# Retention computed in two blocks of 256 tokens with a decayed state between them

## The reference

```python
CHUNK = 64
q = rotary(...) * (C_HEAD_DIM ** -0.5);  k = rotary(...)
d_intra = exp(log_gamma * abs(idx[:, None] - idx[None, :]))       # inside a chunk of 64
k_dec, q_dec = exp(log_gamma * (CHUNK - 1 - idx)), exp(log_gamma * (idx + 1))
scores = einsum('bnthd,bnshd->bnhts', qc, kc) * d_intra
y_intra = einsum('bnhts,bnshe->bnthe', scores, vc)
kv = einsum('bnshd,bnshe->nbhde', kc * k_dec, vc)
state = state * chunk_dec + kv                                    # from chunk to chunk
y_cross = einsum('bnthd,nbhde->bnthe', qc * q_dec, s_prev)
y = y_intra + y_cross     # then normalised per head, times silu(g)
```

## Time and profile before

| | us |
|---|---|
| median of 3 runs | 1739.63 (1738.88 to 1739.86) |
| the profiled execution, its own time | 1739.68 |
| its span in the profile | 1737.7 |
| TensorE busy | 1720.9 (99% of the span) |
| VectorE busy | 1265.9 (73%) |
| ScalarE busy | 768.3 (44%) |
| retention of layer 0, between slabs 10 and 11 | 135.87 to 158.55 |
| retention of layer 1 | 696.22 to 718.90 |

### The profile page before, as it was taken

How to read it: one execution, slowest core, us unless ns; L and a number is a source line. 1 busy time by engine, 2 the same in 40 slices (tenths; PEclk the granted TensorE clock), 3 DMA queues, 4 the chain that set the end, 5 groups by cost and what they waited for, 6 DMA issues and landing times.

```text
span 1737.7 us, 22378 instructions
## 1 busy us (share of the span) xinstructions
PE 1720.9 (99%) x8460; PEld 1392.2 (80%) x8460; DVE 1265.9 (73%) x1788; ACT 768.3 (44%) x1045; POOL 13.9 (1%) x7
## 2 busy tenths in 40 slices
PE   9999999999999999999999999999999999999998
PEld 8886888888888988688888888788766788888886
DVE  6378786876777646878678688766589568777778
ACT  6424442333333523344233233355798474454442
POOL 0000000000000000000000000000000200000000
PEclk9999999999999999999999999999999999999999
DMA  7330334333333233042433433353410223222321
GB/s 291 122 121 25 127 116 145 121 121 137 128 121 121 97 100 119 27 155 101 145 121 119 144 120 121 121 175 124 118 38 2 73 100 116 101 97 97 114 105 49
DMA packets 33351, 195.25 MB, mean 112 GB/s; under 512 B 5760, under 2 KB 7168, under 8 KB 11264
## 3 DMA queue, kind: packets, MB, share of 16 engines
q1 hardware_dynamic: 24656, 156.77, 26.3%
q10 hardware_dynamic: 8624, 37.49, 6.5%
HBM read 187.43 MB, written 2.11 MB: 109 GB/s over the span
## 4 chain that ended last, share of the span: by engine, by line
PE 95%; DVE 2%; ACT 1%; issue 1%; DMA 1%; SPq 0%; DVEq 0%; ACTq 0%; PEldq 0%
PE ps L573 29%; PE ps L574 29%; PE ps L575 29%; PE ps L729 1%; PE ps L743 1%; PE ps L989 1%; PE ps L971 1%; PE ps L1007 1%; DMA raw<-in_weights 1%; PE ps L643 1%; DVE acc L2633 1%; PE ps L751 0%; PE ps L907 0%; DMA x<-in_xin 0%; DVE acc L2643 0%
## 5 line engine op out<-in xcount | busy, mean ns | idle before, releaser
L573 PE MATMUL ps<-xh,wh 128*128 128x512 f32 x1440 | 564.6, 392 | 3.0 <-DVE xl L1858 1.8
L575 PE MATMUL ps<-xh,wl 128*128 128x512 f32 x1440 | 560.5, 389 | 0.0
L574 PE MATMUL ps<-xl,wh 128*128 128x512 f32 x1440 | 560.5, 389 | 0.0
L1173 ACT ACTIVATE wh<-raw 128x2048 fp32r<-128x2048 f32 x128 | 244.5, 1913 | 299.2 <-DMA raw<-in_weights 294.4
L573 PEld LDWEIGHTS ps<-xh,wh 128*128 128x128 f32 x1440 | 270.3, 188 | 63.8 <-issue 7.0
L574 PEld LDWEIGHTS ps<-xl,wh 128*128 128x128 f32 x1440 | 270.4, 188 | 56.7 <-issue 1.2
L575 PEld LDWEIGHTS ps<-xh,wl 128*128 128x128 f32 x1440 | 270.3, 188 | 56.8
L1894 DVE TENSOR_TENSOR wl<-raw,wh 128x2048 fp32r<-128x2048 f32 x110 | 251.5, 2287 | 86.6 <-ACT wh L1173 86.4
L1408 ACT ACTIVATE cv<-upb,prm 128x512 f32<-128x512 f32 x88 | 67.0, 809 | 223.2 <-DVE upb L2094 223.2
L1882 DVE CUSTOM_DVE_ANT_0 adab<-adab,crow 128x1024 f32<-128x1024 f32 x44 | 52.2, 1223 | 130.4 <-DMA adab<-in_ada 130.4
L573 PE MATMUL ps<-wh,xh 128*128 128x256 f32 (+1 forms) x288 | 97.0, 337 | 0.0
(11 more groups left out here) (323 smaller groups left out, 2427.2 us busy)
## 6 DMA issues: line engine op xcount, KB each, us to landing
raw<-in_weights SPq DMA_DIRECT2D x129, 1024.0 KB, 4.9
adab<-in_ada ACTq DMA_DIRECT2D x22, 1024.0 KB, 4.9
both<-in_weights SPq DMA_DIRECT2D x7, 2048.0 KB, 7.7
t<-in_cst ACTq DMA_DIRECT2D x1, 3200.0 KB, 10.3
x<-in_xin SPq DMA_DIRECT2D x8, 256.0 KB, 5.8
turned<-q ACTq DMA_DIRECT2D x8, 256.0 KB, 4.1
turned<-k ACTq DMA_DIRECT2D x8, 256.0 KB, 4.2
adab_tail<-in_ada ACTq DMA_DIRECT2D x2, 1024.0 KB, 9.6
```

The source lines that it names most:

```text
L573: pe.matmul(out, w_hi, m_hi, start=start, stop=False)
L574: pe.matmul(out, w_hi, m_lo, start=False, stop=False)
L575: return pe.matmul(out, w_lo, m_hi, start=False, stop=stop)
L1173: act.activation(wh[:, s, :], raw[:, s, :], ACT.Copy).then_inc(hi_made, 1)
```

## The change

The 512 tokens are cut into two blocks of 256. Scores are made inside a block only: key tiles 0 and 2 against 256 query tokens, key tiles 1 and 3 against 128. What the second block sees of the first comes through a state of 64 x 64 per head: the sum over the first block's keys, each times gamma^(256-s), times the values. It is made once per layer, kept by ScalarE, and multiplied with the second block's queries, each times gamma^(t-256), into the same accumulators as the values. For this the first 256 keys are turned (8 transposes, behind slab 9), VectorE multiplies them (`kd`) and the queries (`qd`) with two new small tables, and the table `decay` has half its width. Scores use banks 0, 1, 4, 5 in two units with two signals; VectorE's multiply takes both tiles of a unit in one instruction. The semaphore `vc_ready` is renamed `ret_operands` and counts the centred values (2), `kd` (2) and `qd` (1).

```diff
@@ -125,9 +126,12 @@
     lg = np.log1p(-np.exp2(-5.0 - np.arange(RET_HEADS)))
-    dist = np.abs(t[None, :] - p[:, None])
-    ok = t[None, :] // CHUNK >= p[:, None] // CHUNK
+    ahead = t[None, :BLOCK]
+    dist = np.abs(ahead - p[:, None])
+    ok = ahead // CHUNK >= p[:, None] // CHUNK
     put(c1, C1, "decay", np.stack([np.where(ok, np.exp(g * dist), 0.0) * HD ** -0.5 for g in lg], 1))
+    put(c1, C1, "q_decay", np.stack([np.exp(lg[2 * i + p // HD][:, None] * ahead) * HD ** -0.5 for i in range(4)], 1))
+    put(c1, C1, "k_decay", np.stack([np.exp(lg[None, :] * (BLOCK - j * P - p)[:, None]) for j in range(2)], 1))
     tb = np.arange(BANDW)
...
@@ -213,10 +219,10 @@
         turned = keep("turned", [P, 4, S])
-        keep("gap", [P, 1024])
+        sT = at("sT", [P, 2, 2, 3 * BLOCK], F32, st_at)
+        assert st_at + size([P, 2, 2, 3 * BLOCK]) == top[0]
+        qd = keep("qd", [P, 4, BLOCK])
         pooled = keep("pooled", [P, 2, S])
-        sT = at("sT", [P, 2, 2, 1280], F32, st_at)
-        assert st_at + size([P, 2, 2, 1280]) == top[0]
         q_at = top[0]
...
@@ -224,6 +230,8 @@
         vss = keep("vss", [P, 3, NT])
+        kd = keep("kd", [P, 2, S])
+        state = keep("state", [P, 4, HD])
         mix_end = top[0]
...
@@ -411,10 +419,10 @@
         mix_bank = (0, 4, 2, 6)
-        s_units = ((0,), (1, 3), (2,))
-        s_banks = ((0, 1), (4, 5), (6, 7), (4, 5))
-        s_cols = (0, 0, 0, 384)
-        soffs = (0, 512, 1024, 896)
+        s_units = ((0, 2), (1, 3))
+        s_banks = ((0, 1), (4, 5), (0, 1), (4, 5))
+        s_cols = (0, 0, BLOCK, P)
+        soffs = (0, 2 * BLOCK, BLOCK, 2 * BLOCK + P)
         var_bank = (3, 3, 6, 7)
...
@@ -663,6 +671,12 @@
 
+                def turn_keys():
+                    for j in range(2):
+                        for p in range(4):
+                            last = pe.transpose(ps[:, 4 + j, p * P:(p + 1) * P], k[:, p, tokens(j)], ident)
+                        last.then_inc(s_done, 1)
+
                 def pool_products():
...
@@ -704,6 +718,11 @@
 
+                    if c == 9:
+                        evacuated(8)
+                        pe.wait_ge(rope_done, l * 2 + 2)
+                        turn_keys()
+
                     if c == 5:
...
@@ -721,27 +740,33 @@
                         if p:
-                            pe.wait_ge(sT_ready, l * 12 + 3 * (p - 1) + n + 1)
+                            pe.wait_ge(sT_ready, l * 8 + 2 * (p - 1) + n + 1)
                         for j in unit:
-                            w = S - j * P
+                            w = BLOCK - j % 2 * P
                             for hh in range(2):
                                 h = slice(HD * hh, HD * hh + HD)
                                 last = pe.matmul(ps[:, s_banks[j][hh], s_cols[j]:s_cols[j] + w], k[h, p, j * P:(j + 1) * P],
-                                                 q[h, p, j * P:S], start=True, stop=True)
+                                                 q[h, p, j * P:j * P + w], start=True, stop=True)
                         last.then_inc(s_done, 1)
 
+                def block_state():
+                    for p in range(4):
+                        for j in range(2):
+                            for hh, h in enumerate(halves):
+                                w = slice(p * P + HD * hh, p * P + HD * hh + HD)
+                                last = pe.matmul(ps[h, 6, p * HD:(p + 1) * HD], kd[:, j, w], vr[:, j, w], start=(j == 0), stop=(j == 1))
+                    last.then_inc(pv_done, 1)
+
                 def ret_values(p):
-                    pe.wait_ge(sT_ready, l * 12 + 3 * p + 3)
-                    if p == 0:
-                        pe.wait_ge(vc_ready, l * 2 + 2)
-                    if p:
-                        pe.wait_ge(y_evac, l * 4 + p)
-                    for j in (0, 1, 3, 2):
-                        w = S - j * P
-                        for hh in range(2):
-                            h = slice(HD * hh, HD * hh + HD)
-                            last = pe.matmul(ps[h, 2, j * P:S], vr[:, j, p * P + HD * hh:p * P + HD * hh + HD],
-                                             sT[:, p % 2, hh, soffs[j]:soffs[j] + w], start=(j == 0), stop=(j == 2))
+                    pe.wait_ge(sT_ready, l * 8 + 2 * p + 2)
+                    pe.wait_ge(y_evac, l * 5 + p + 1)
+                    for j in range(NT):
+                        w = BLOCK - j % 2 * P
+                        for hh, h in enumerate(halves):
+                            pe.matmul(ps[h, 2, j * P:j * P + w], vr[:, j, p * P + HD * hh:p * P + HD * hh + HD],
+                                      sT[:, p % 2, hh, soffs[j]:soffs[j] + w], start=(j % 2 == 0), stop=(j == 1))
+                    for h in halves:
+                        last = pe.matmul(ps[h, 2, BLOCK:S], state[h, p, :], qd[h, p, :], start=False, stop=True)
                     last.then_inc(pv_done, 1)
...
@@ -750,10 +775,10 @@
 
-                evacuated(8)
                 evacuated(9)
                 pe.wait_ge(pooled_ready, l * 2 + 2)
-                pe.wait_ge(rope_done, l * 2 + 2)
+                pe.wait_ge(ret_operands, l * 5 + 5)
+                block_state()
                 ret_scores(0)
...
@@ -1296,6 +1321,9 @@
                         ahead(7, n0, n3)
+                    if c == 10:
+                        act.wait_ge(pv_done, l * 5 + 1)
+                        act.activation(state[:, :, :], ps[:, 6, 0:4 * HD].rearrange("p (i d) -> p i d", i=4), ACT.Copy).then_inc(y_evac, 1)
                     if c in (9, 10):
...
@@ -1988,22 +2016,27 @@
                 evacuate(9, sg, 0)
+                for j in range(2):
+                    dve.wait_ge(s_done, l * 10 + j + 1)
+                    dve.tensor_tensor(kd[:, j, :].rearrange("p (h d) -> p h d", d=HD), bank(4 + j).rearrange("p (h d) -> p h d", d=HD),
+                                      k_decay[:, j, :].rearrange("p (h a) -> p h a", a=1).broadcast_to((P, RET_HEADS, HD)),
+                                      ALU.mult).then_inc(ret_operands, 1)
+                dve.tensor_tensor(qd[:, :, :], q[:, :, BLOCK:S], q_decay, ALU.mult).then_inc(ret_operands, 1)
                 ahead(9)
                 evacuate(10, sg, 2)
 
                 def decayed(p):
 
-                    if l or p >= 2:
-                        dve.wait_ge(pv_done, l * 4 + p - 1)
-                    for n, unit in enumerate(s_units):
-                        dve.wait_ge(s_done, l * 12 + 3 * p + n + 1)
-                        for j in unit:
-                            b0, b1 = s_banks[j]
-                            w = S - j * P
-                            last = dve.tensor_tensor(sT[:, p % 2, :, soffs[j]:soffs[j] + w],
-                                                     ps[:, b0:b1 + 1, s_cols[j]:s_cols[j] + w],
-                                                     decay[:, 2 * p:2 * p + 2, 0:w], ALU.mult)
-                        last.then_inc(sT_ready, 1)
+                    if p >= 2:
+                        dve.wait_ge(pv_done, l * 5 + p)
+                    for n, w in enumerate((BLOCK, P)):
+                        b0, b1 = s_banks[n]
+                        at = soffs[n]
+                        dve.wait_ge(s_done, l * 10 + 2 * p + n + 3)
+                        dve.tensor_tensor(sT[:, p % 2, :, at:at + 2 * w].rearrange("p h (j t) -> p h j t", j=2),
+                                          ps[:, b0:b1 + 1, 0:2 * w].rearrange("p h (j t) -> p h j t", j=2),
+                                          decay[:, 2 * p:2 * p + 2, 0:w].rearrange("p h (a t) -> p h a t", a=1).broadcast_to((P, 2, 2, w)),
+                                          ALU.mult).then_inc(sT_ready, 1)
 
```

More of the change, by code:

```diff
@@ L26 @@
 RET_HEADS = 8
+BLOCK = S // 2
 EPS = 1e-6
@@ L95 @@
 for _name, _w in (("ident", P), ("ones", P), ("head_mean", P), ("cos", S), ("sin", S),
-                  ("decay", RET_HEADS * S), ("band", 2 * 4 * BANDW)):
+                  ("decay", RET_HEADS * BLOCK), ("q_decay", 4 * BLOCK), ("k_decay", 2 * RET_HEADS), ("band", 2 * 4 * BANDW)):
     C1[_name] = (_at, _w)
@@ L203, in build @@
         decay = c1("decay").rearrange("p (h t) -> p h t", h=RET_HEADS)
+        q_decay = c1("q_decay").rearrange("p (i t) -> p i t", i=4)
+        k_decay = c1("k_decay").rearrange("p (j h) -> p j h", j=2)
         band = c1("band").rearrange("p (f g t) -> p f g t", f=2, g=4)
@@ L351, in build @@
         pv_done, y_evac = sem("pv_done"), sem("y_evac")
-        vsum_ready, vc_ready, gsq_ready = sem("vsum_ready"), sem("vc_ready"), sem("gsq_ready")
+        vsum_ready, ret_operands, gsq_ready = sem("vsum_ready"), sem("ret_operands"), sem("gsq_ready")
         var_ready, gr_ready, gsd_ready = sem("var_ready"), sem("gr_ready"), sem("gsd_ready")
@@ L1327, in keep_values @@
                 def keep_values(p):
-                    act.wait_ge(pv_done, l * 4 + p + 1)
+                    act.wait_ge(pv_done, l * 5 + p + 2)
```

(4 more changed lines are left out.)

## The result

| | before | after |
|---|---|---|
| median, us | 1739.41 (1738.88 to 1740.48, 6 runs) | 1729.93 (1729.21 to 1730.52, 6 runs) |
| span of the profiled execution, us | 1737.7 | 1727.7 |

The ratio of the times is 0.9945, 95% interval 0.9935 to 0.9955.

A forecast was written before the change was run, and what follows sets the result against it. The prediction took TensorE to bound the kernel. Per layer, -3.4 (scores), -1.0 (values), +0.9 (transposes) and +1.1 (state) made -2.4 to -2.5 us, -4.9 in both: 1739.6 to 1734.7 us, range 1732.8 to 1738.4.

The forecast's parts named there:

- Scores: TensorE's score products in the retention: 1.51 us per group for 2.36, saving 3.4 us a layer.
- values: TensorE's value products with the state product: 2.04 us for 2.30, saving 1.0 us a layer.
- transposes: Eight added key transposes on TensorE behind slab 9: 0.88 us a layer.
- state: The added block_state products on TensorE, 16 with heads side by side: 1.1 us a layer.
- The change of shape: TensorE's switch to the state product's third weight shape: between 0 and 0.23 us, 0.16 charged.
- Serial state pairs: Rival: the two heads' state products run one after the other, +3.4 us, 1738.1 us; chance 0.17.
- new wait: Rival: one of two narrow spots in the stage missed by about 1 us per layer, 1736.7 us; chance 0.13.
- VectorE's idle time: The gap before the next slab's low part, said to hide kd and qd with 2.3 us left.
- the bound: Rival: the repeated table slows VectorE's decay until it bounds the stage; at three times, 1754.6 us; chance 0.04.
- The first part of decay 1: Narrow spot on VectorE: needed by scores 2, ready with 0.7 us to spare.
- Variance 1: Narrow spot on TensorE: needs ScalarE's root of pair 0, with 1.2 us remaining.
- The step that failed: Claim that tables from memory, 0.5 MB smaller and used some 100 us after loading, have no effect.

The follow-up runs named there:

- e2: The changed kernel with 64 bytes left free behind the tables t1, so the layers' buffers behind them lie 64 bytes further; 1734.57 us.
- f3: The changed kernel with the state held per head in 128 partitions, zeros in the other head's, and qd read over all partitions; 1727.99 us.
- h1: The kernel before with 32 bytes left free behind t1, shifting the layers' buffers behind it; 1742.00 us.
- e3: The kernel before with only ah and al moved, 64 bytes down; 1741.32 us.
- e1: The kernel before with 64 bytes left free behind t1, shifting every buffer of the layers behind it; 1734.62 us.
- e4: The kernel before with everything from the first buffer on moved 64 bytes, and the layers' buffers behind t1 by 64 more; 1735.13 us.
- h2: The changed kernel with q, k, vr, sg and what lies behind them 128 bytes further, ah and al left in place; 1729.67 us.

## Why the prediction was right in the stage and wrong in the sum

- **Scores, values, transposes, state.** All four terms, and the stage net of them, came out as forecast (above): 1.51, 2.03, 0.87 and 1.08 us for 1.51, 2.04, 0.88 and 1.1. Net of the stage and the transposes: 19.26 + 0.87 - 22.68 = -2.55 us in layer 0, and the same from 690.88 to 710.14 in layer 1; -2.4 to -2.5 was forecast. e2 shows the whole of it as a time, with the MLP's products as slow in sum as before: 1734.57 for 1734.7.
- **The change of shape**, with the shape itself, costs the state product 0.15 us (f3), between the bounds 0 and 0.23.
- **Serial state pairs** did not happen. Were they serial, the two records of each head with 256 columns would make 4 x 0.21 = 0.85 us and the change of shape; it is 0.58. In the starts of the trace the two heads' first records lie 7 ns apart (144.321 and 144.328), and so do their second ones (144.588 and 144.595). The two heads write different partitions of one bank at the same time. The Trainium skill, TensorEngine Tiling, section "Gotcha 1: PSUM Pressure", says that different row tiles cannot access the same PSUM bank at once. The 0.58 us speak against it for this form, and the trace decides.
- **No new wait.** TensorE is busy for 19.60 of 19.60 us in the stage, at a granted clock of 1.00 (busy time by stretch, after; it answers to the earlier trace rows):

```profile
136.50:156.10 19.60, 19.60 (x186) 12.23 (x185) 14.68 (x16) 10.06 (x16) 0.00 (x0) 1.00 0.17 54
```

  VectorE and ScalarE after, in the stage (start, length, engine, line, operation, idle before and what ended it); they answer to the earlier trace rows:

```profile
127.17 1.28 DVE L2021 TENSOR_TENSOR kd<-ps,t 128x512 f32<-128x512 f32 x2
128.36 1.22 DVE L2024 TENSOR_TENSOR qd<-q,t 128x1024 f32<-128x1024 f32 x1
132.11 2.29 DVE L1922 TENSOR_TENSOR wl<-raw,wh 128x2048 fp32r<-128x2048 f32 x1 [2.53 <-ACT wh L1198]
...
142.86 1.81 DVE L2036 TENSOR_TENSOR sT<-ps,t 128x1024 f32<-128x1024 f32 x2
...
152.49 3.34 DVE L2044 RECIPROCAL k<-k 128x512 f32<-128x512 f32 x1
```

```profile
151.13 0.69 ACT L1372 ACTIVATE k<-ps,eps 128x512 f32<-128x512 f32 x1
153.15 0.60 ACT L1358 ACTIVATE y<-ps 128x512 f32<-128x512 f32 x1 [1.33 <-PE ps L769]
```

  `kd` and `qd` fit into VectorE's idle time, of which 2.53 us are left (2.3 forecast). Both tiles in one instruction with the repeated table take 1.81 us for 1536 elements, so VectorE did not become the bound. The first part of decay 1, which starts at 142.86, ends at 144.07, 0.8 us ahead of scores 2 at 144.90 (0.7 forecast). Variance 1 starts at 153.03, 1.2 us behind the root (151.13 + 0.69), as forecast. The reciprocals start 3.6 us before slab 11, for 3.9 forecast.
- **The step that failed** is the sentence "The tables from memory shrink by 0.5 MB, used some 100 us after they are loaded: no effect." I looked at the tables as a transfer and not as what stands in front of all other buffers. With it the sum took the rest of TensorE's list to cost what it had cost. It was worth 4.7 us: 4032 bytes took the distance of `ah` and `wh` from 192 to 0 modulo 256. That the edit hit 0 was luck: with 64 bytes more the same change gains 5.0 us (e2). The trace of the kernel before already held the sign, and I did not follow it: the groups by form of the whole run have the second and third product of a sum (L574, L575) at 389 ns on `xh` and `xl`, and at 394 in three of the four groups on `ah` and `al`.

What stays open is why the distance counts. In the traces the load of the next product's weights starts 2 to 4 ns behind each of these products and takes 188 ns, so both operands are read at the same time. That the two reads meet in the same part of the memory or not would fit; it is argued only. No run changed one read and left out the other. Nor does the table tell a product's own weights from those of the next product, for inside a slab both stand at the same distance. They differ only where slabs meet in layer 1. In h1 the last product on `xh` has its own weights at 0 and the next ones (`ah`) at 32, and takes 235 ns (10 times); the last one on `wh` has its own at 32 and the next at 0, and takes 226 (9 times). There the next weights count. But the same two places have 232 and 232 ns in e3, and 226 and 229 in e2, which neither reading explains. Nor is it known why at 64 bytes the three products differ among each other, and at the other distances not.

## What to carry to other kernels

When TensorE is the bound, list its products by form over the whole run and compare the mean of one between groups of the same shape: a few nanoseconds on a thousand products were as much as the whole change here. When an edit changes the size of a buffer, work out where every buffer behind it comes to lie, and compare the products of both kernels outside the edited stage before the gain is put down to the edit. Removing columns from small products paid what their distance from start to start said, and the further shape of weights took 0.15 us of it back each time.

## What the runs showed of the hardware that was not expected

- A float32r product of 128 x 128 weights and 512 columns starts 227 ns after its neighbour if the addresses of its moving operand and its weights differ by a multiple of 256 bytes, and 232 to 234 ns at 32, 128, 192 and 224; at 64 one product in three is as fast as at 0, and the mean is 229. Over 1056 products this was 4.7 us of 1739, and 7 us in h1 against e1 (1742.00 and 1734.62, on different chips; 233.3 and 226.8 ns in the traces). The granted clock was 0.999 in both.
- Where each operand stands by itself, modulo 128 bytes, made no difference (e4 against e1: 1735.13 and 1734.62).
- Plain float32 products with 128 x 64 weights did not feel a distance of 128 bytes (h2: 1.451 us for a group, as after).
- Two products with weights of 64 partitions by 64 columns, in opposite corners, ran side by side into one bank: 0.58 us for a pair of heads with 256 columns each, their records 7 ns apart.
